# Low parts of the projection weights by accumulating transfers onto a negated high part

## The reference

```
h = rmsnorm(x, norm_w[l])
proj = einsum('bld,de->ble', h, w_in[l])            # 1024 x 3592, float32
(s5_x, s5_g, hg_q, hg_f, hg_i, hg_g, ml_q, ..., rt_g) = split(proj)
mixed = concat([s5_out * silu(s5_g), hg_out * silu(hg_g), ml_out * silu(ml_g), rt_out * silu(rt_g)])
x = x + einsum('ble,ed->bld', mixed, w_out[l])
```

## Time and profile before

| | |
|---|---|
| median of 3 runs | 1563.61 us (1559.76, 1563.61, 1570.64) |
| span of the profiled execution | 1568.8 us, 1.8 us below the slowest of these |
| TensorE matmul busy | 1385.4 us |
| VectorE busy | 888.5 us |
| ScalarE busy | 551.4 us |
| GpSimd busy | 451.0 us |
| mean granted TensorE clock | 0.926 |

### The profile page before, as it was taken

The page is one execution under the profiler, slowest core; times in us unless marked ns, Lnnn a source line. Parts: engine busy times, 40 slices in busy tenths (PEclk is TensorE's granted clock), DMA queues, the critical chain, the costliest instruction groups (busy, mean ns, idle before and its releaser), DMA issues.

```text
span 1568.8 us, 31689 instructions
## 1 busy us (share of the span) xinstructions
PE 1385.4 (88%) x12391; PEld 1213.8 (77%) x12391; DVE 888.5 (57%) x2670; ACT 551.4 (35%) x1197; POOL 451.0 (29%) x628
## 2 busy tenths in 40 slices
PE   2869899989897898878999989998999899789896
PEld 2758788878776888866887879977878898779665
DVE  5986757463795526444746544656465444653637
ACT  4445343343323423322442344332642443331011
POOL 4332434431002443222210145452200444231001
PEclk9978899989897999988999999997999899889999
DMA  6223123431233432363322333341313415344501
GB/s 174 95 81 70 55 83 108 141 107 63 70 111 106 118 76 77 96 87 82 115 67 82 107 107 110 108 141 58 116 54 116 109 57 123 123 115 89 157 9 58
DMA packets 167563, 149.84 MB, mean 96 GB/s; under 512 B 63440, under 2 KB 155352, under 8 KB 165752
## 3 DMA queue, kind: packets, MB, share of 16 engines
q1 hardware_dynamic: 96696, 76.38, 18.1%
q10 hardware_dynamic: 70720, 71.44, 15.4%
HBM read 124.42 MB, written 23.37 MB: 94 GB/s over the span
## 4 chain that ended last, share of the span: by engine, by line
PE 64%; DVE 17%; ACT 6%; issue 5%; DMA 3%; POOL 3%; SPq 1%; DVEq 0%; ACTq 0%; POOLq 0%
PE psum L2384 18%; PE psum L2389 17%; PE psum L2718 5%; DVE r L1723 4%; PE psum L2637 3%; DVE r L2097 3%; PE psum L2696 2%; PE psum L2636 2%; PE psum L2548 2%; PE psum L2456 2%; ACT r L1504 1%; POOL rs L1214 1%; PE psum L2634 1%; POOL wlo L1189 1%; DVE QE L2118 1%
## 5 line engine op out<-in xcount | busy, mean ns | idle before, releaser
L1189 POOL TENSOR_TENSOR wlo<-wraw,whi 128x256 fp32r<-128x256 f32 (+1 forms) x448 | 351.6, 820 | 415.6 <-ACT whi L1233 415.6
L2389 PE MATMUL psum<-whi,hhi 128*128 128x256 f32 (+1 forms) x896 | 273.5, 305 | 13.2 <-ACT th L1320 11.1
L2389 PE MATMUL psum<-wlo,hhi 128*128 128x256 f32 (+1 forms) x896 | 264.2, 295 | 0.0
L2389 PE MATMUL psum<-whi,hlo 128*128 128x256 f32 (+1 forms) x896 | 264.0, 295 | 0.0
L2384 PE MATMUL psum<-hhi,whi 128*128 128x288 f32 (+2 forms) x672 | 232.5, 346 | 6.3 <-ACT r L1354 4.1
L2384 PE MATMUL psum<-hlo,whi 128*128 128x288 f32 (+2 forms) x672 | 221.4, 329 | 5.1 <-issue 5.1
L2384 PE MATMUL psum<-hhi,wlo 128*128 128x288 f32 (+2 forms) x672 | 220.9, 329 | 0.0
L2389 PEld LDWEIGHTS psum<-whi,hhi 128*128 128x128 f32 x896 | 182.4, 204 | 20.8 <-issue 11.8
L2389 PEld LDWEIGHTS psum<-wlo,hhi 128*128 128x128 f32 x896 | 182.7, 204 | 0.7 <-issue 0.5
L2718 PE MATMUL psum<-wraw,mixT 128*128 128x256 f32 x768 | 179.5, 394 | 3.3 <-DVE xo L2314 3.3
L2389 PEld LDWEIGHTS psum<-whi,hlo 128*128 128x128 f32 x896 | 181.9, 203 | 0.0
(11 more groups left out here) (355 smaller groups left out, 2323.5 us busy)
## 6 DMA issues: line engine op xcount, KB each, us to landing
wraw<-in_w_in ACTq DMA_DIRECT2D x50, 1024.0 KB, 5.4
wraw<-in_w_out ACTq DMA_DIRECT2D x14, 1024.0 KB, 5.5
x<-xo SPq DMA_DIRECT2D x48, 128.0 KB, 2.3
r<-x SPq DMA_DIRECT2D x10, 512.0 KB, 5.5
r<-in_c_rot SPq DMA_DIRECT2D x4, 1088.0 KB, 7.3
wraw<-in_w_in ACTq DMA_DIRECT2D x4, 1056.0 KB, 5.6
r<-WTm SPq DMA_DIRECT2D x4, 1024.0 KB, 11.0
r<-VTm SPq DMA_DIRECT2D x4, 1024.0 KB, 5.9
```

What stands on the lines that cost most here:

```text
L1189: nc.gpsimd.tensor_tensor(wlo[:, hslot[b], ks, 0:width], wraw[:, wslot[b], ks, 0:width], whi[:, hslot[b], ks, 0:width].bitcast(F32), ALU.s ...
L2389: mm = nc.tensor.matmul(bank.t[:, 0:width], x[:, kt, c], w[:, sl, kt, 0:width], start=first, stop=last)
```

## The change

`EARLY`, a list of blocks whose low part GpSimd still subtracts, is empty: no block has subtracts. For each of the 56 blocks ScalarE, behind the Copy into `whi`, waits for its end and writes `wlo` = -whi with a second Copy of scale -1. GpSimd waits for this (`wneg_done`) and issues two transfers with an adding destination, from `wraw` onto `wlo`, each over half of the k-tiles (128 partitions of 4 KB, 512 KB). TensorE and the next load wait for these transfers (`wlo_sum`, by half). In the first piece of a block that isn't a sample piece TensorE does all products with `whi` first and those with `wlo` behind them, half a piece at a time where a piece is cut in two; the sample piece has no wait for a low part. The weight tiles lie without gaps.

```
@@ split_low (GpSimd)
                 b = blocks.pop(0)
+                width = BLOCK[b[1]][2]
+                if b in by_dma:
+                    pool.wait_ge(*wneg_done.at(b))
+                    for h in range(2):
+                        c = slice(h * KT // 2 * width, (h + 1) * KT // 2 * width)
+                        nc.gpsimd.dma_start(wlo[:, hslot[b], c].bitcast(F32), wraw[:, wslot[b], c], accum_op=ALU.add).then_inc(*wlo_sum[hslot[b], h].inc(b))
+                    return
                 prev = before(in_blocks, b, 2)
...
@@ split_high (ScalarE)
-                nc.scalar.activation(whi[:, hslot[b], :, 0:width], wraw[:, wslot[b], :, 0:width], ACT.Copy).then_inc(*whi_done.inc(b))
+                c = slice(0, KT * width)
+                nc.scalar.activation(whi[:, hslot[b], c], wraw[:, wslot[b], c], ACT.Copy).then_inc(*whi_done.inc(b))
+                if b in by_dma:
+                    act.wait_ge(*whi_done.at(b))
+                    nc.scalar.activation(wlo[:, hslot[b], c], whi[:, hslot[b], c].bitcast(F32), ACT.Copy, scale=-1.0).then_inc(*wneg_done.inc(b))
@@ load_until (ScalarE)
                         act.wait_ge(*whi_done.at(prev))
-                        act.wait_ge(*wlo_done.at(prev + (KT - 1,)))
+                        for kt in (KT // 2 - 1, KT - 1):
+                            act.wait_ge(*wlo_ready(prev, kt))
@@ projection (TensorE)
-                            if k == pieces_of_block(*b)[0]:
-                                pe.wait_ge(*wlo_done.at(b + (kt,)))
...
+                            new = k == [q for q in pieces_of_block(*b) if not tiled(q)][0]
+                            three = ((hhi, whi), (hhi, wlo), (hlo, whi))
+                            order = [(kt, x, w) for kt in kts for x, w in three]
+                            if new:
+                                order = [o for o in order if o[2] is whi] + [o for o in order if o[2] is wlo]
+                            for kt, x, w in order:
+                                if new and w is wlo:
+                                    pe.wait_ge(*wlo_ready(b, kt))
```

More of the change, by code:

```diff
@@ L521, in trunk_kernel, with weights @@
         hlo = sb("hlo", [P, KT, W], F32R)
-        wraw = sb("wraw", [P, 2, KT, WC])
-        with nc.sbuf_tensor("tail_w", [P, 2, KT, WC], F32) as tail_w:
-            pass
-        whi = sb("whi", [P, 2, KT, WC], F32R)
-        wlo = sb("wlo", [P, 2, KT, WC], F32R)
+        wraw = sb("wraw", [P, 2, KT * WC])
+        with nc.sbuf_tensor("tail_w", [P, 2, KT * WC], F32) as tail_w:
+            pass
+        whi = sb("whi", [P, 2, KT * WC], F32R)
+        wlo = sb("wlo", [P, 2, KT * WC], F32R)
+        def weights(buf, slot, width=256):
+            return buf[:, slot, 0:KT * width].rearrange("p (k c) -> p k c", k=KT)
         mixT = sb("mixT", [P, 10, W])
@@ L729, in trunk_kernel, with wlo_ready @@
         whi_done = signal("whi_done", in_blocks)
-        wlo_done = signal("wlo_done", [b + (g,) for b in in_blocks for g in range(KT)])
+        by_pool = [b for b in in_blocks if b in EARLY]
+        by_dma = [b for b in in_blocks if b not in EARLY]
+        wneg_done = signal("wneg_done", by_dma)
+        wlo_sub = signal("wlo_sub", [b + (g,) for b in by_pool for g in range(KT)])
+        wlo_sum = {(a, h): signal(f"wlo_sum{a}{h}", [b for b in by_dma if hslot[b] == a], 16) for a in range(2) for h in range(2)}
+        def wlo_ready(b, kt):
+            return wlo_sub.at(b + (kt,)) if b in by_pool else wlo_sum[hslot[b], kt * 2 // KT].at(b)
         th_keys = [k for k in pieces if BLOCK[k[1]][4] == "av"]
@@ L2369, in _ @@
                                     pe.wait_ge(*PB[bank_of[u]].free.at(u))
-                        for kt in range(*((0, 4) if part[0] == "mm" else (4, KT)) if long_piece(k) else (KT,)):
-                            if k == pieces_of_block(*b)[0]:
-                                pe.wait_ge(*wlo_done.at(b + (kt,)))
-                            if tiled(k):
-                                width = BLOCK[b[1]][2] // 4
+                        kts = range(*((0, 4) if part[0] == "mm" else (4, KT)) if long_piece(k) else (KT,))
@@ L2375, in _ @@
+                        width = BLOCK[b[1]][2]
+                        if tiled(k):
+                            width //= 4
+                            for kt in kts:
                                 for g in range(4):
-                                    mm = nc.tensor.matmul(bank.t[TS * g:TS * g + TS, 0:width], mixT[:, kt, HALF:W], wraw[:, wslot[b], kt, g * width:(g + 1) * width],
+                                    mm = nc.tensor.matmul(bank.t[TS * g:TS * g + TS, 0:width], mixT[:, kt, HALF:W], weights(wraw, wslot[b], 4 * width)[:, kt, g * width:(g + 1) * width],
@@ L2377, in _ @@
                                                           start=kt == 0, stop=kt == KT - 1)
-                                continue
-                            for x, w in ((hhi, whi), (hhi, wlo), (hlo, whi)):
-                                first, last = kt == 0 and w is whi and x is hhi, kt == KT - 1 and x is hlo
+                        else:
+                            new = k == [q for q in pieces_of_block(*b) if not tiled(q)][0]
[6 more added lines that the diff above has]
+                                    pe.wait_ge(*wlo_ready(b, kt))
+                                first, last = kt == 0 and w is whi and x is hhi, (kt, x, w) == order[-1] and kt == KT - 1
+                                wv = weights(w, sl, width)
@@ L2390, in _ @@
-                        if kt == KT - 1:
+                                    mm = nc.tensor.matmul(bank.t[:, 0:ln], wv[:, kt, k[2] * P:(k[2] + 1) * P], x[:, kt, c0:c0 + ln], start=first, stop=last)
+                                else:
+                                    mm = nc.tensor.matmul(bank.t[:, 0:width], x[:, kt, k[2] * P:k[2] * P + P], wv[:, kt, :], start=first, stop=last)
+                        if kts[-1] == KT - 1:
                             mm.then_inc(*bank.full.inc(k))
```

26 lines of the change are left out of this document (10 added, 16 removed).

## The result

The changed kernel takes 1550.2 us (median of 11 runs, 1540.1 to 1554.9), the kernel before 1562.5 us (11 runs, 1555.7 to 1570.6). The ratio is 0.991, 95% interval 0.9885 to 0.9934: 12 us faster by the medians, 14 by the ratio (10 to 18), 0.9%. The forecast was 1554, 9.7 us faster. Sum and measurement lie close together by luck: two terms behind the sum were far off and cancelled, which is what the experiments are about. Times are therefore compared by their ratio to it, and a difference of two ratios is uncertain by 5 to 8 us either way. A trace shows one execution.

A forecast was written before the change was run, and what follows sets the result against it. TensorE, busy 88% of the span, was taken as nearly the bound, waiting for VectorE's and ScalarE's mixer steps. Terms -18-9.7+13+5 = -9.7 us, from a median of 1563.6, gave 1554 us, range 1528 to 1590.

The forecast's parts named there:

- a median landing over 7 us: Sign against the forecast: accumulating halves were expected to land in a median near 5.5 us; over 7 would prove it wrong.
- subtracts leave: VectorE no longer stands behind GpSimd's reads, -18 us, and the chain no longer passes over GpSimd's queued subtracts, -9.7 us.
- second copy on ScalarE: 56 more activations of 1.9 us delay evacuations and gate tanh queued behind them: 8 us on the chain, 5 off it, +13.
- transfers: Late landings make TensorE wait, 3 us, and ScalarE stand before loads, 2 us: +5 us, bounds 0 and 60.
- order and layout: Matmul order and contiguous weight layout change neither count nor columns on TensorE: nothing.
- what is late next: With VectorE freed, the first stretch counts its whole 9 us; in the mixer TensorE's projections come next, two thirds, 9.
- Rival (a): More comes back: all of 23 and 9.7 us, ScalarE's off-chain cost and landings nothing; -25 us, 1539; 23%.
- a half lands in 5.5 us: Each 512 KB accumulating transfer lands 5.5 us after issue, between a store's 3.2 and a read's 10.7.
- Rival (b): Slower by late landings: a half at 10.7 us gives +40 in place of +5, net +25, 1589; 20%, 4 for late issue.
- The way into it by VectorE's locks: Each GpSimd issue waits out a 1.2 us VectorE instruction, all 2.4 us later: net about +7, 1571; 4%.
- Their later issue costs nothing: The next weight loads, issued later behind the wait for sums, have a whole block's time: no cost.
- The third place on GpSimd's queue: Subtracts of 5.65 us at 1223.38 ahead of sample piece L2376, which waits no longer: gains all 5.6 us.

The follow-up runs named there:

- e5: The changed kernel with neither transfers nor second copy, TensorE multiplying zeros as low parts: 1500.3 us, ratio 0.9586 to the kernel before.
- e10: The kernel with subtracts only, each subtract replaced by a GpSimd memset of the same length, TensorE reading whi for wlo: 1513.7 us, ratio 0.9684 to before.
- e3: The changed kernel without its 112 transfers, the second copy on ScalarE kept: 1511.6 us, ratio 0.9687 to the kernel before.
- e4: The changed kernel without the second ScalarE copy, transfers kept and issued right behind the first copy: 1523.4 us, ratio 0.9761 to the kernel before.
- e1: The changed kernel with subtracts for all blocks again, matmul order and contiguous layout kept: 1557.3 us, ratio 0.9994 to the kernel before.
- e6: The changed kernel with TensorE reading whi for wlo and not waiting for transfers, loads still waiting: 1540.2 us, ratio 0.9834 to the kernel before.
- e9: The changed kernel with each transfer moving 128 KB instead of 512, all copies, issues and waits kept: 1522.8 us, ratio 0.9742 to the kernel before.

## Why the prediction was right, and where its terms were wrong

The sign and the size came out: 9.7 us forecast, 12 to 14 measured, in the range 1528 to 1590. This was luck. The gain of the subtracts' leaving was 37 us larger than forecast and the loss by the transfers 30 us larger, and nothing in the prediction made the one weigh up the other. By one of its own signs, a median landing over 7 us, it was wrong. By its own steps:

| step | predicted | shown by the runs |
|---|---|---|
| subtracts leave | -27.7 (18 VectorE, 9.7 queue) | -65 (58 to 71): e5; 49 of it VectorE: e10 |
| second copy on ScalarE | +13 | +16 alone (e3 less e5), +23 beside the transfers (e4) |
| transfers | +5, ends 0 and 60 | +35 (e3); +27 without the copy (e5 to e4) |
| order and layout | 0 | none seen (e1: -1, interval -4 to +2) |
| sum | -9.7 | -65 + 16 + 35 = -14 (steps from before to e5, e3 and the changed kernel, which add up by construction) |

**The step "what is late next" on the subtracts failed (term: 18 us for VectorE, measured 49).** I found the mechanism and its size per instruction: the forms went to 755, 190 and 175 ns as said, and seven r products (L2136 now) take 1.50 us at 117.58 in VectorE's timeline, as the earlier trace rows had promised. But I priced only what the chain showed, 23 us, and took a third off the mixer's part, which left 18. VectorE's busy time fell by 72 us in all, and without the reads (e10) the kernel is 49 us faster. The chain is one path. That the stretched instructions off it held up steps just behind the chain, which become the chain once it is shortened, is how I explain the rest; no run shows it step by step. Rival (a), "more comes back", spoke of this and stopped at -32.7, because it too was bounded by the chain.

A part of the 49 us is **TensorE's clock**, which I had not priced. The windows view (stretch, length, busy time and count of PE, PEld, DVE, ACT, POOL, then granted clock, DMA share, GB/s), kernel before first:

```profile
40.00:80.00 40.00, 35.63 (x189) 30.39 (x188) 37.34 (x108) 16.03 (x21) 16.33 (x21) 0.96 0.28 90
...
120.00:160.00 40.00, 36.38 (x345) 32.32 (x345) 28.03 (x76) 21.98 (x40) 12.68 (x17) 0.90 0.27 65
160.00:200.00 40.00, 34.24 (x367) 30.19 (x366) 25.45 (x81) 15.55 (x33) 15.93 (x22) 0.87 0.18 54
```

Then the changed kernel:

```profile
120.00:160.00 40.00, 35.82 (x366) 29.39 (x366) 27.96 (x110) 27.88 (x40) 6.05 (x8) 1.00 0.59 129
160.00:200.00 40.00, 37.70 (x357) 35.22 (x357) 16.05 (x54) 21.21 (x45) 5.99 (x8) 0.91 0.52 134
```

Then e5, without low parts:

```profile
120.00:160.00 40.00, 39.72 (x448) 33.76 (x450) 25.39 (x100) 24.19 (x41) 2.75 (x5) 1.00 0.27 80
160.00:200.00 40.00, 37.40 (x324) 34.22 (x322) 20.12 (x64) 19.02 (x50) 2.49 (x4) 1.00 0.26 82
```

Before, TensorE is idle for 3.6 and 5.8 of these 40 us, and the granted clock is at its lower level (1.2 GHz) for part of both; in e5 it is at the higher level (2.4 GHz) throughout, with 0.3 and 2.6 us idle. The sum of idle time in a stretch does not decide it: the changed kernel is idle for 4.2 us from 120 to 160 at the higher level throughout, and for 2.3 us from 160 to 200 with 0.91. The stretches don't hold the same matmuls, so I compare whole kernels: TensorE's busy time times the mean granted clock is nearly the same in all thirteen traces, 1277 to 1287 us (before 1385.4 x 0.926 = 1283, after 1378.2 x 0.934 = 1287, e5 1356.0 x 0.944 = 1280, e10 1358.2 x 0.946 = 1285). So busy time falls only by the clock. Between the traces of the kernel before and of e10, 27 of the 57 us of span that went are TensorE's busy time and 30 its idle time; in the changed kernel 7 of 16. But the trace of the kernel before is of its slowest execution. By the median clock of all runs beside e10 (0.932 before, 0.944 in e10) the same product gives 17 of the 49 us, an estimate: about a third came as clock, and the rest as idle time that went. Kernels with less idle time have the higher clock by and large (e3, e4, e5, e9 and e10, idle for 146 to 158 us, have 0.940 to 0.947), but not one by one: e6 is idle for 176 us at 0.942, the changed kernel for 175 at 0.934. What moved the clock is not shown; no run varied it by itself.

**The step "a half lands in 5.5 us" failed, and with it the +5.** Measured 7.7 us median, 4.7 to 21.2. I had said that I am wrong over 7. TensorE's waits for it, of the source view of the issue's line (us, times; PEld and PE rows overlap in time):

```profile
who waited for it (us, times):
  PEld psum L2419: 16.3, 10
  PE psum L2419: 14.1, 10
  PEld psum L2417: 7.5, 2
  PE psum L2417: 6.8, 2
```

That is 21 us of TensorE's idle time, of which e6 shows 12 to decide. Rival (b) had the landing waits right: for a half of 7 to 8 us it gave shortfalls of 18 us. Its +40 was for a half of 10.7 us, and that the transfers cost 35 at a half of 7.7 comes from elsewhere, since 23 of them are there with no wait on TensorE. It was also wrong in what stood against them, since its gain was 27.7 and not 65. The way into it by VectorE's locks (by its own terms +10 and not +7, as 2.4 us go at two places of the queue) did not come: 112 issues take 1.06 us each on the mean (850 to 1242 ns in the source view), near the 1.0 that I took, with VectorE's 576-element products at 755 ns beside them. The rule that the prediction took for it speaks of VectorE's two-port instructions, and no row had shown these products to be such. The Trainium skill ("SBUF — State Buffer", Who interferes with whom) says that a VectorE instruction with two SBUF inputs contends with a GpSimd instruction that reads SBUF and not with one that only writes it. e10 agrees (819.1 against 888.5 us). The Trainium skill's fit for a plain transfer (a fitted 2.0 us plus bytes over 436 GB/s, "DMA: Bandwidth & Descriptors") gives 3.2 us for these 512 KB, an estimate; the measured 7.7 is more than twice that, and 128 KB took 4.2 where the fit gives 2.3.

**"Their later issue costs nothing" failed.** I gave the loads a whole block's time and looked at their own wait alone. Of the transfers' 35 us, 23 are there with no TensorE wait at all (e6). The waits of ScalarE for the raw weights and for the reads of x, from the view of who waited for whom (us, times, longest), in the changed kernel:

```profile
ACT whi L1255 <- DMA wraw<-in_w_in: 43.1, 7, 10.3
...
ACT th L1298 <- DMA r<-x: 9.5, 3, 6.7
```

and in e6:

```profile
ACT whi L1255 <- DMA wraw<-in_w_in: 57.4, 10, 10.0
```

and in e3, without transfers:

```profile
ACT whi L1251 <- DMA wraw<-in_w_in: 38.3, 7, 10.5
...
ACT th L1294 <- DMA r<-x: 5.4, 2, 3.7
```

The kernel before has 31.2 us in 4 cases for the weights, but e1, which has subtracts too, has 38.4 in 6, so this wait alone tells little between the kernels; only e6 stands out. What is slower is plainer in the landings. The median of a read of x went from 5.5 to 8.4 us. The 56 loads of w_in take 7.3 us on the mean in the changed kernel, 6.3 before and 6.2 in e3, and 15 of them take over 8 us, where 6 and 3 do. So other transfers are slower while the transfers' 58.9 MB move on a queue of their own, and e9 says the same from the other side (26 us for three quarters of the bytes). ScalarE's own stops at the wait for a sum are small: 9.5 us in five cases, where it stopped 7.8 us in four for the subtracts. How the 23 us divide between slowed reads, weight loads issued later because they wait for the sums, and ScalarE standing at that wait with evacuations behind it, stays open: a kernel whose loads don't wait for the sums would overwrite wraw under a transfer, and this was not tried.

**ScalarE's second pass held.** +13 forecast, +16 alone (8 to 24). At 134.18 the chain shows the two pieces of 1.92 and 1.93 us, and GpSimd's queue at 24.62 holds 1.92 + 1.98 where 4.0 was said. Beside the transfers it is 23, where it also puts each landing 1.9 us later; the difference of 7 is within the noise.

**The third place on GpSimd's queue** (5.6 us at 1223.38) was wrong in its reason: in e1 the sample piece waits no longer either, and the subtracts stand on the chain there for 10.3 us ahead of an rs. What the place is worth can't be told by itself. The comparison of e10 and e5 leaves 16 us for it, for the other two places and for TensorE's waits, against the 9.7 and a part of the 3 that I counted. One sign failed for a simple reason: GpSimd's busy time fell by 251 us and not by 350, because its issues count as busy, 101 us.

## What to carry to other kernels

Where two engines disturb each other, take the whole of the stretched instructions' extra busy time as the upper end, not the part on the chain: here it was 72 us, 23 were on the chain, and the kernel gained 49, about a third of them (an estimate) as TensorE's clock. When work is moved from an engine to DMA, charge the bytes to every transfer in flight beside them and to the loads that wait behind, with one experiment that cuts the bytes and keeps the waits. And move only the blocks where the disturbance bites: without the first four of 56 blocks the whole gain was gone, and the first eight alone gave twice the change's gain.

## What the runs showed of the hardware that was not expected

An accumulating SBUF transfer is dear. Half a block (512 KB) landed in 7.7 us at the median and 128 KB in 4.2 us; the queue that carries them moved 58.9 MB and took 19.9% of the 16 engines' time, where the weight loads' queue moved 71.4 MB in 15.2%, so a byte took 1.6 times as long. No plain transfer of this size and route was run, so how much of it is the adding is not shown. GpSimd spent 1.06 us on each issue, 101 us in all, which is more than a quarter of the time of the subtracts that it replaced.

GpSimd's memsets of 823 ns left VectorE's 2670 instructions at 819 us, its subtracts of 820 ns stretched them to 888.5; GpSimd's own instruction took the same time in both.

TensorE's busy time for the same 12391 matmuls went from 1385.4 to 1356.0 us with the granted clock (mean 0.926 to 0.944), as its idle time went from 183 to 146 us (traces of the kernel before and of e5).
